# Two-layer hybrid backbone with a top-2-of-8 expert layer: the residual's scale and shift moved from the router stage to the tail, and the router's order changed

## The reference, cut to what matters

```python
x = layer_norm(ALPHA * x + g1 * mix, ln_g[1, 0], ln_b[1, 0])   # output of the convolution sub-layer
h = x * (1 + sc2) + sh2                                         # what the experts see
logits = h @ w_router; top_logit, top_e = top_k(logits, 2); gates = softmax(top_logit)
y[token] = sum over its 2 experts of gate * swiglu_expert(h)    # 8 experts, hidden width 3584
x = layer_norm(ALPHA * x + g2 * y, ln_g[1, 1], ln_b[1, 1])      # the result
```

## Time and profile before

| | |
|---|---|
| median of 3 runs | 2247.52 us (2244.53 to 2247.78) |
| the profiled execution | 2246.7 us, span 2245.1 us, mean granted clock 0.978 |
| busy | PE 96%, PE weight loads 76%, DVE 67%, ACT 50%, POOL 16% |
| router stage in the trace | about 916 to 957 us from the span's start |
| expert loop | about 957 to 2197 us |
| tail | 2197 to 2245 us |

### The profile page before, as it was taken

How to read it: one execution, slowest core, us unless ns; L and a number is a source line. 1 busy time by engine, 2 the same in 40 slices (tenths; PEclk the granted TensorE clock), 3 DMA queues, 4 the chain that set the end, 5 groups by cost and what they waited for, 6 DMA issues and landing times.

```text
span 2245.1 us, 33136 instructions
## 1 busy us (share of the span) xinstructions
PE 2146.2 (96%) x12156; PEld 1715.7 (76%) x12157; DVE 1493.3 (67%) x1391; ACT 1131.6 (50%) x1278; POOL 368.8 (16%) x247
## 2 busy tenths in 40 slices
PE   6999999999999999799799999999999999999994
PEld 4876688887888888678677788888888887666882
DVE  3456656667457544789566645459999997555984
ACT  4135536222224522377555534347888885445872
POOL 0030004999991000100000000000000000000001
PEclk8999999999999999799899999999999999999997
DMA  8472022555443222399577755559999996557974
GB/s 328 195 293 83 1 97 100 188 189 200 168 179 120 76 93 102 142 375 371 197 275 271 306 197 184 193 183 410 367 395 378 384 370 251 211 218 269 380 292 158
DMA packets 78098, 515.87 MB, mean 230 GB/s; under 512 B 9008, under 2 KB 9264, under 8 KB 20944
## 3 DMA queue, kind: packets, MB, share of 16 engines
q1 hardware_dynamic: 61696, 442.85, 51.3%
q0 software_dynamic: 16336, 72.11, 8.5%
HBM read 482.41 MB, written 32.51 MB: 229 GB/s over the span
## 4 chain that ended last, share of the span: by engine, by line
PE 88%; DVE 6%; issue 2%; ACT 1%; DMA 1%; SPq 0%; POOL 0%; DVEq 0%; ACTq 0%; POOLq 0%
PE ps L1851 25%; PE ps L1853 24%; PE ps L1852 24%; PE ps L2232 3%; PE ps L2296 2%; PE ps L603 2%; PE ps L558 2%; PE ps L614 2%; PE ps L2278 1%; DVE lo L1191 1%; PE ps L1910 1%; PE ps L562 1%; DVE fl L1495 1%; DMA raw_pair<-w_mod 1%; PE ps L2029 0%
## 5 line engine op out<-in xcount | busy, mean ns | idle before, releaser
L1851 PE MATMUL ps<-ah,hi 128*128 128x512 f32 (+1 forms) x768 | 286.8, 373 | 5.7 <-DVE al L1356 2.4
L1853 PE MATMUL ps<-ah,lo 128*128 128x512 f32 (+1 forms) x768 | 284.9, 371 | 0.0
L1852 PE MATMUL ps<-al,hi 128*128 128x512 f32 (+1 forms) x768 | 284.9, 371 | 0.0
L1439 DVE TENSOR_TENSOR lo<-raw,hi 128x2048 fp32r<-128x2048 f32 x112 | 255.8, 2284 | 0.0
L1439 DVE TENSOR_TENSOR loa<-raw_pair,hia 128x2048 fp32r<-128x2048 f32 x112 | 251.1, 2283 | 1.1 <-ACT hia L960 1.1
L1439 DVE TENSOR_TENSOR lob<-raw_pair,hib 128x2048 fp32r<-128x2048 f32 x112 | 251.7, 2283 | 0.0
L960 ACT ACTIVATE hia<-raw_pair 128x2048 fp32r<-128x2048 f32 x112 | 214.4, 1915 | 49.9 <-DMA raw_pair<-w_moe 49.8
L1191 DVE TENSOR_TENSOR lo<-raw_pair,hi 128x2048 fp32r<-128x2048 f32 x59 | 183.8, 3118 | 80.0 <-ACT hi L848 78.5
L960 ACT ACTIVATE hi<-raw 128x2048 fp32r<-128x2048 f32 x112 | 214.8, 1918 | 11.1 <-DMA raw<-w_moe 11.1
L1851 PE MATMUL ps<-hia,xth 128*128 128x512 f32 x504 | 204.2, 405 | 16.2 <-issue 14.6
L960 ACT ACTIVATE hib<-raw_pair 128x2048 fp32r<-128x2048 f32 x112 | 215.0, 1921 | 1.0 <-DMA raw_pair<-w_moe 0.9
(11 more groups left out here) (309 smaller groups left out, 4050.0 us busy)
## 6 DMA issues: line engine op xcount, KB each, us to landing
raw_pair<-w_moe SPq DMA_DIRECT2D x224, 1024.0 KB, 6.7
raw<-w_moe SPq DMA_DIRECT2D x112, 1024.0 KB, 6.8
raw_pair<-w_pre SPq DMA_DIRECT2D x59, 1024.0 KB, 4.8
raw_pair<-w_mod SPq DMA_DIRECT2D x20, 1024.0 KB, 7.2
raw_pair<-w_mod POOLq DMA_DIRECT2D x14, 1024.0 KB, 5.2
rawm<-w_mod POOLq DMA_DIRECT2D x14, 1024.0 KB, 5.5
dispatched_x<-zt POOLq DMA_DIRECT2D x22, 512.0 KB, 10.8
xg<-dispatched_x POOLq DMA_DIRECT2D x8, 1024.0 KB, 11.3
```

Of the source, the lines that this page charges most:

```text
L1439: dve.tensor_tensor(LO_OF[j], raw8(r), HI_OF[j].bitcast(F32), ALU.subtract).then_inc(raw_used[r], 1)
L1851: pe.matmul(outp, wh, ah, start=first, stop=False, skip_group_check=True)
L1852: pe.matmul(outp, wh, al, start=False, stop=False, skip_group_check=True)
L1853: return pe.matmul(outp, wl, ah, start=False, stop=last, skip_group_check=True)
```

## The change

- PE and DVE: the two residual spreads and the eight residual instructions leave the router stage and stand in the tail, ahead of the wait for `dg_ready` on PE and behind `DG` on DVE. `XR` keeps the plain normalised rows through the expert loop.
- PE: positions come ahead of `spread(6,1)`; `rows(1)` comes between them. The wait for `xr_ready` is gone.
- DVE: positions and destinations come ahead of all four `row_tile`s. `back_ready` is signalled after the gates `GA` and no longer after `BACK`. `low_part(3)` comes after the four `token_tiles`.
- ACT: the wait for `routed` ahead of the Silu table is gone.
- Tail: the g2 spread goes to banks 4,5 (they were 0,1), the mix starts at banks 6,7 and goes round; PE waits for `dga_ready` before the g2 spread and for `xr_ready` before the second tile of the mix.

```diff
@@ ACT
-            act.wait_ge(routed, 1)
             act.wait_ge(unit_done[2], t.n(("hs", 2)))
             act.preload_act_table(ACT.Silu)
...
-            act.activation(G2R[:]..., PS[:, 0:2, :], ACT.Copy).then_inc(g2_ready, 1)
+            act.activation(G2R[:]..., PS[:, 4:6, :], ACT.Copy).then_inc(g2_ready, 1)
@@ DVE
-            dve.wait_ge(spread_full, 2)
-            row_tile(0)
             dve.wait_ge(pos_full, 1)
...
             dve.tensor_copy(DI[:], DF[:]).then_inc(dest_ready, 1)
-            for i in range(1, 4):
+            dve.wait_ge(spread_full, 2)
+            for i in range(4):
                 row_tile(i)
...
-            dve.tensor_copy(BACK[:], DF[:]).then_inc(back_ready, 1)
+            step(dve.tensor_copy(BACK[:], DF[:]))
...
-            step(dve.tensor_tensor(GA[:, 1, :], DD[:, 1, :], GA[:, 0, :], ALU.mult))
-            dve.wait_ge(spread_full, 4)
-            dve.wait_ge(ht_ready, 4)
-            for i in range(4):
-                ins = affine_tile(XR, i, 2, 4)
-            ins.then_inc(xr_ready, 1)
+            dve.tensor_tensor(GA[:, 1, :], DD[:, 1, :], GA[:, 0, :], ALU.mult).then_inc(back_ready, 1)
...
             low_part(2)
-            low_part(3)
             for i in range(4):
                 token_tiles(i)
+            low_part(3)
...
             ins.then_inc(dg_ready, 1)
+            dve.wait_ge(spread_full, 4)
+            for i in range(4):
+                ins = affine_tile(XR, i, 0, 2)
+            ins.then_inc(xr_ready, 1)
...
-                b = (2 * i + 2) % 8
+                b = (2 * i + 6) % 8
@@ PE
             spread(0, 0)
-            pe.wait_ge(shift_ready, 5)
-            spread(6, 1)
             pe.wait_ge(tr_free, 1)
             pe.wait_ge(mask_ready, 1)
...
             ins.then_inc(pos_full, 1)
-            for i in range(1, 4):
+            rows(1)
+            pe.wait_ge(shift_ready, 5)
+            spread(6, 1)
+            for i in range(2, 4):
                 rows(i)
             pe.wait_ge(tr_free, 4)
-            spread(2, 2)
-            spread(4, 3)
-            pe.wait_ge(xr_ready, 1)
             pe.wait_ge(routed, 1)
...
+            spread(0, 2)
+            spread(2, 3)
             pe.wait_ge(dg_ready, 1)
+            pe.wait_ge(dga_ready, 1)
             for k in range(KD):
-                ins = pe.matmul(PS[:, k // 4, ...], mean_w, DG[:, k, :], ...)
+                ins = pe.matmul(PS[:, 4 + k // 4, ...], mean_w, DG[:, k, :], ...)
             ins.then_inc(g2_full, 1)
-            pe.wait_ge(dga_ready, 1)
             for i in range(4):
                 pe.wait_ge(yg_in[i], 32)
+                if i == 1:
+                    pe.wait_ge(xr_ready, 1)
                 if i == 3:
                     pe.wait_ge(g2_ready, 1)
...
-                        ins = pe.matmul(PS[:, (2 * i + 2) % 8 + b, :], DGA[:, 2 * i + c, :], ...)
+                        ins = pe.matmul(PS[:, (2 * i + 6) % 8 + b, :], DGA[:, 2 * i + c, :], ...)
```

More of the change, by code:

```diff
@@ L1170, in _ @@
             act.wait_ge(g2_full, 1)
-            act.activation(G2R[:].rearrange("p (b n) -> p b n", b=2), PS[:, 0:2, :], ACT.Copy).then_inc(g2_ready, 1)
+            act.activation(G2R[:].rearrange("p (b n) -> p b n", b=2), PS[:, 4:6, :], ACT.Copy).then_inc(g2_ready, 1)
             for i in range(4):
@@ L2373, in _ @@
                     expert(2, x + (NE + 1), None)
+            spread(0, 2)
+            spread(2, 3)
             pe.wait_ge(dg_ready, 1)
+            pe.wait_ge(dga_ready, 1)
             for k in range(KD):
-                ins = pe.matmul(PS[:, k // 4, (k % 4) * P:(k % 4 + 1) * P], mean_w, DG[:, k, :], start=True, stop=True,
+                ins = pe.matmul(PS[:, 4 + k // 4, (k % 4) * P:(k % 4 + 1) * P], mean_w, DG[:, k, :], start=True, stop=True,
                                 skip_group_check=True)
             ins.then_inc(g2_full, 1)
-            pe.wait_ge(dga_ready, 1)
             for i in range(4):
                 pe.wait_ge(yg_in[i], 32)
+                if i == 1:
+                    pe.wait_ge(xr_ready, 1)
                 if i == 3:
@@ L2387, in _ @@
                     for c in range(2):
-                        ins = pe.matmul(PS[:, (2 * i + 2) % 8 + b, :], DGA[:, 2 * i + c, :],
+                        ins = pe.matmul(PS[:, (2 * i + 6) % 8 + b, :], DGA[:, 2 * i + c, :],
                                         YG[i][c][:, 512 * b:512 * b + 512], start=(c == 0), stop=(c == 1),
```

## The result

The changed kernel takes 2268.73 us (median of 4 runs, 2264.33 to 2269.71), the kernel before 2246.67 in the same comparison (4 runs, 2244.53 to 2247.78): ratio 1.0099, interval 1.0087 to 1.0111. It is **22 us slower**, and the forecast of 2243.0 (2240.0 to 2246.2) does not hold it. The profiled execution took 2269.21, span 2267.6, mean clock 0.972, so the span grew by 22.5.

A forecast was written before the change was run, and what follows sets the result against it. PE was taken to bound the loop, DVE and DMA close behind. First product -4.3, weights +0.2, tail 0: -4.1 us, giving 2242.6 from the profiled execution or 2243.4 from the median; 2243.0 named, range 2240.0 to 2246.2.

The forecast's parts named there:

- Rival B: Loop start: code load queues behind weights, another 11.10 us stall (2254.1), chance 0.06; or stall at 1080.80 halved (2237), 0.07.
- Step 1: Router stage: positions ahead of the second spread start at about 920.8 instead of 922.5; DI ready 1.9 us sooner.
- Step 2: Router stage: row tiles wait for the second spread; first done at 929.9, last at 937.0, 0.6 us later.
- Step 3: POOL's queue: scatter starts 0.3 us behind first tile, ends about 1.05 late; XG issued at 943.7, lands at 949.05.
- Rival C: POOL's scatter is late by only 0.3 us, so PE starts 5.0 us sooner: 2242.2, chance 0.15.
- Step 4: PE's transposes ahead of the first expert begin at 949.1 instead of 951.91, 2.8 us sooner, still cold.
- the prediction's own sign: Wrong if transposes start after 950, ACT waits over a microsecond for early weights, or DVE's first mix waits for `xr_ready`'s work.
- Step 5: DVE's order before the first expert: first product at 952.6 instead of 956.91, 4.3 us sooner; low part 3 hidden.
- Step 6: SP's weight loads start later, at 951.0, but barely hold: 0.2 us lost; afterwards DMA catches up.
- rival A: Weights bound the loop's start: units 2 us late cut the gain to 2.3 us, 2245.2; chance 0.15.
- Step 7: Moved signals: `back_ready` comes 0.7 us after BACK, costing nothing.
- Step 8: Tail: the moved residual fits while DVE idles, done 7 us ahead of the first mix result; cost 0.

The follow-up runs named there:

- experiment 3: Kernel before with only the residual's spreads and instructions moved to the tail, plus 128 padding waits on PE restoring the placement: 2240.60 us against 2245.14.
- experiment 7: experiment 3 with ACT's wait for `routed` dropped and low part 3 put behind the four token tiles: 2238.85 us against 2245.14 of the kernel before.
- experiment 8: experiment 7 with SP's first weight loads waiting for the landed scatter instead of XG: 2239.73 us against 2245.14 of the kernel before.
- experiment 1: Changed kernel with 128 satisfied waits (64 instructions) added on PE, restoring the old loop placement: 2245.06 us against 2245.14 of the kernel before.

## Why the prediction was wrong

The sign of the forecast, the size and the range were wrong, and one step failed for most of it.

- **Rival B, code loading: the right mechanism at the wrong place and price.** The prediction said that PE's stream is 64 instructions shorter and that its blocks fall elsewhere, but it asked only for a block "first asked for after SP's loads", at the first expert, priced it at 11.1 and gave it 0.06. The first expert pays nothing. The code that is fetched anew is wanted on the way to the third expert, where weights fill the queues: seven packets and four branches that take 22.1 us for 0.2 each before. PE idles 21.08, and 23.0 are lost in all. The sum had no term for this. The argument against ("PE stands before `xg_in`") holds only for code reached in sequence. What the rows offered was a stall at 1080.80 at the second expert and none in a later one, 1504 to 1626: a sign that some branches of this loop cost this much and others nothing. From it a loss of one more such stall per kind of branch should have had a real chance, and the size should have been left open upwards. The other half of B, a shorter stall at 1080.80, is wrong too: 11.20 for 11.10.
- **Step 1** holds. Positions start 1.65 us sooner (forecast 1.7), `DI` is done 1.57 sooner (1.9).
- **Steps 2 and 3, the scatter, were mis-sized: 1.05 late was forecast for XG, 3.21 came.** PE's and DVE's timelines of the kernel after, then POOL's:

```profile
920.60 2.37 PE L2191 MATMUL ps<-mm,rt 128*128 128x8 f32 x20
...
923.72 1.79 PE L2172 MATMUL ps<-small,xz 128*128 128x128 f32 x8
925.31 2.91 PE L2179 MATMUL ps<-small,coef 128*128 128x128 f32 x16
```

```profile
926.25 0.17 DVE L1666 CAST di<-df 128x8 uint32<-128x8 f32 x1
928.26 1.22 DVE L1642 TENSOR_TENSOR ht<-xr,ps 128x1024 f32<-128x1024 f32 x1 [1.84 <-PE ps L2179]
```

```profile
931.63 1.06 POOL L799 DMA_INDIRECT dispatched_x<-ht,di  x1 [250.71 <-DVE ht L1643]
...
940.62 0.96 POOL L799 DMA_INDIRECT dispatched_x<-ht,di  x1 [0.30 <-issue]
945.64 0.77 POOL L820 DMA_DIRECT2D xg<-dispatched_x  x1 [4.06 <-DMA dispatched_x<-ht,di]
```

  The row tiles wait for the second spread. `rows(1)`, put ahead of it, takes 1.79 at a clock of 0.54 where 0.9 was taken, and the spread 2.91 for 2.6. The first tile starts at 12.12 on the table's scale; the forecast's 927.4 is 11.0. POOL begins 0.9 after tile 0 is done, not 0.3. And the wait behind the last issue is 4.06, not 3.57. These are 1.1 + 0.6 + 0.5 = 2.2, the difference. The step had named the right chain, with each link at its shortest price. What it calls 2.6 warm was itself taken at a mean clock of 0.67 (917.3 to 922.5). Rival C, a scatter that isn't late, is out with this.
- **Step 4.** The transposes start 0.5 us sooner and not 2.8: 35.01 for 35.52. It is step 3's 2.2 handed on; the load took 5.5 us from issue to PE, near the 5.35 taken. Wrong by the prediction's own sign, since 951.15 lies behind its 950:

```profile
951.15 3.63 PE L2216 MATMUL ps<-small,xg 128*128 128x128 f32 x16 [21.18 <-DMA xg<-dispatched_x]
```

- **Step 5** holds in itself: the first product follows the transposes' start by 3.30 us (3.5 forecast, 5.00 before), and low part 3 behind the turned rows costs nothing that shows. The gain of 4.3 became 2.2 only by step 4.
- **Step 6 and rival A.** ACT waits for weights in the first groups, 0.92 and 0.87 us:

```profile
966.07 1.92 ACT L960 ACTIVATE hi<-raw 128x2048 fp32r<-128x2048 f32 x1 [0.92 <-DMA raw<-w_moe]
...
969.34 1.92 ACT L960 ACTIVATE hib<-raw_pair 128x2048 fp32r<-128x2048 f32 x1 [0.87 <-DMA raw_pair<-w_moe]
```

  They cost PE nothing here: its first expert takes 122.34 us for 122.32 before. In experiments 3 and 7, where the first product comes sooner, such waits did cost 1.3 and 2.7 (experiment 8). So A is no part of this result, but its mechanism is real.
- **What step 6 calls afterwards** was missing a term: 1.1 of the 2.2 us is given back by the second expert. Behind the stall of 11 us the clock came back later. Windows of the kernel before, then of the one after (the stall ends at 1091.9 and at 1089.6; the clock is the third number from the end):

```profile
1094.00:1095.00 1.00, 1.00 (x4) 0.76 (x4) 0.00 (x0) 0.00 (x0) 0.00 (x0) 0.58 1.00 406
1095.00:1096.00 1.00, 1.00 (x6) 0.82 (x5) 0.00 (x0) 0.00 (x0) 0.00 (x0) 1.00 0.90 369
```

```profile
1093.00:1094.00 1.00, 1.00 (x4) 0.71 (x4) 0.00 (x0) 0.00 (x0) 0.00 (x0) 0.50 0.62 242
1094.00:1095.00 1.00, 1.00 (x5) 0.82 (x4) 0.00 (x0) 0.00 (x0) 0.00 (x0) 0.71 0.00 0
```

  Full speed is back 3 us behind the stall in the one, 5 in the other; two microseconds at half speed are one of work.
- **Steps 7 and 8** hold. Nobody waits for the moved signals. In the tail the residual is far ahead of the first mix result, as forecast. Timeline of DVE:

```profile
2235.06 1.22 DVE L1643 TENSOR_TENSOR xr<-xr,ps 128x1024 f32<-128x1024 f32 x1
2242.55 1.23 DVE L1808 TENSOR_TENSOR zf<-ps,g2r 128x1024 f32<-128x1024 f32 x1 [6.26 <-PE ps L2386]
```

  6.3 us of cover remain where 7 were counted. The tail is 0.96 longer all the same, because the first mix step comes at 22.41 behind `DG` and not at 21.45; in experiments 1 and 3 the tail takes 0.44 and 0.57 more than before, in experiment 8, with the same tail, 0.05. The step's 0 was thus short by up to one microsecond, which differs from run to run; no run takes this apart.

With the placement kept (experiment 1) the gain of 4.1 us did not come either: the ratio is 0.9999, which on the 2246.67 of the result is 2246.4 (2244.2 to 2248.5), at the upper bound of the range or past it. The errors of steps 3, 6 and 8 are sizes and use the gain up; that of rival B makes the kernel 1% slower.

**Still open:** why a shift of 16 instructions one way makes two branches long, 32 to 128 four, and 32 the other way stalls six experts; which blocks they are; why POOL began 0.9 us behind row tile 0; and why the clock came back later behind the same stall. No run tried to separate these.

## What to carry to other kernels

Where a long loop branches over the code of several cases, any edit ahead of it also moves its code. Here that alone cost 22 us. Compare the count of instruction packets, the "issue" stalls and the length of PE's branches before and after, and time the edit again with padding that restores the placement before judging it. Moving the residual behind the loop was worth 4.5 us here (6.3 with ACT's wait and the low part) and looked like a loss of some 20. And before a wait is moved ahead of other work, follow who waits for what it was moved past: the destinations came sooner, but the rows they were for came later.

## What was not expected of the hardware

- 16 instructions of shift cost 9.74 us of standing at the third expert, 32 the other way made the kernel 128 us slower (2374.70 for 2246.33), with 100 code packets for 46.
- A branch of PE that takes 0.2 us in one placement takes 2 to 8 us in another, under weight traffic; stalls of 6 to 30 us are two to six of them in a row. DVE and ACT run out of work meanwhile (busy for 3.35 and 2.01 of 19.60).
- A wait instruction whose semaphore is long reached takes PE's sequencer 109 ns (192 of them from 940.3 to 961.1).
- Clock behind an 11 us stall: back at its upper level (2.4 GHz) after 3.1 us in the kernel before, after 5.2 in the kernel after and after 4.3 to 6.0 in the other ones, with the same matmuls.
